# One channel group of the last convolution span moved to GpSimd, and the work between projections and attention put in another order

## The reference, cut to what matters

```python
mod = silu(c) @ ada_w + ada_b                    # 6 x 1024: shift1, scale1, gate1, shift2, scale2, gate2
h = rms_norm(x, norm_mix) * (1 + scale1) + shift1
q, k, v, u = split(h @ w_in)                     # 8 query heads, 2 key heads, head size 64
q, k = apply_rope(rms_norm(q)), apply_rope(rms_norm(k))
attn_out = softmax(q k^T / 8) v
val, gate = split(u); a = val * sigmoid(gate)
y = depthwise_conv(a, conv_w) + conv_b           # 512 channels, 31 taps
conv_out = silu(layer_norm(y, conv_ln_g, conv_ln_b))
x = x + gate1 * (concat([attn_out, conv_out]) @ w_out)
x = x + gate2 * expert_choice_ffn(rms_norm(x, norm_ffn) * (1 + scale2) + shift2)   # 16 experts
```

## Time and profile before

| what | us |
|---|---|
| runs of the kernel, median of 3 (lowest, highest) | 1512.67 (1510.94, 1512.75) |
| the profiled execution, its own time | 1508.8 |
| its span, first to last instruction | 1507.0 |
| PE busy | 1418.2 (94%) |
| DVE busy | 1106.1 (73%) |
| ACT busy | 798.6 (53%) |
| POOL busy | 209.9 (14%) |

### The profile page before, as it was taken

One profiled execution on the slowest core, in us unless ns is written; L12 is line 12 of the kernel. 1 busy time (PEld: TensorE's weight loads), 2 busy tenths in 40 slices (PEclk: granted clock), 3 DMA queues, 4 the chain that ended last, 5 costly groups with the idle time before them and its releaser, 6 DMA issues.

```text
span 1507.0 us, 26861 instructions
## 1 busy us (share of the span) xinstructions
PE 1418.2 (94%) x9933; PEld 1066.8 (71%) x9933; DVE 1106.1 (73%) x1564; ACT 798.6 (53%) x1303; POOL 209.9 (14%) x211
## 2 busy tenths in 40 slices
PE   4999999978999998998499999999999999999996
PEld 1777787636887886876277777777777777777774
DVE  1258888988877887437678887778877787877884
ACT  2222222136777775223556766566665666756662
POOL 0022022100000000211102111221012210212110
PEclk8999999989999999999599999999999999999998
DMA  9400001273000001333888888989889898889951
GB/s 361 153 1 28 29 1 56 98 293 114 2 2 2 2 2 56 112 131 130 300 303 295 299 296 289 317 290 305 287 301 313 290 308 283 304 290 315 308 186 18
DMA packets 113682, 281.31 MB, mean 187 GB/s; under 512 B 10581, under 2 KB 16825, under 8 KB 110552
## 3 DMA queue, kind: packets, MB, share of 16 engines
q1 hardware_dynamic: 105944, 259.54, 48.2%
q0 software_dynamic: 7680, 20.98, 6.0%
HBM read 259.51 MB, written 20.97 MB: 186 GB/s over the span
## 4 chain that ended last, share of the span: by engine, by line
PE 88%; DVE 5%; DMA 2%; ACT 1%; POOL 1%; SPq 1%; issue 1%; DVEq 0%; ACTq 0%; POOLq 0%
PE banks L1455 12%; PE banks L1460 12%; PE banks L1456 12%; PE banks L1480 12%; PE banks L1135 9%; PE banks L1338 6%; PE banks L1146 6%; PE banks L1287 4%; PE banks L1262 4%; PE banks L1272 4%; DVE c_t L1677 2%; DMA ada<-in_ada_w 1%; PE banks L1510 1%; PE banks L1487 1%; PE banks L1299 1%; DMA xn_sample<-xn 1%
## 5 line engine op out<-in xcount | busy, mean ns | idle before, releaser
L2003 DVE TENSOR_TENSOR low<-raw,high 128x1024 fp32r<-128x1024 f32 x384 | 446.5, 1218 | 1.0
L985 ACT ACTIVATE high<-raw 128x1024 fp32r<-128x1024 f32 x384 | 380.4, 1051 | 9.6 <-issue 8.8
L1677 DVE SCALAR_TENSOR_TENSOR c_t<-a_t,taps,c_t 128x256 f32<-128x256 f32 (+2 forms) x360 | 215.0, 660 | 0.5
L1455 PE MATMUL banks<-high,x_hi 128*128 128x512 f32 x512 | 207.9, 406 | 0.0
L1456 PE MATMUL banks<-high,x_lo 128*128 128x512 f32 x512 | 200.5, 392 | 0.0
L1460 PE MATMUL banks<-low,x_hi 128*128 128x512 f32 x512 | 158.3, 390 | 1.1 <-DVE low L2003 1.1
L1135 PE MATMUL banks<-h_t,w_u 128*128 128x256 f32 x640 | 143.9, 382 | 2.9 <-ACT h_t L735 2.9
L1135 PEld LDWEIGHTS banks<-h_t,w_u 128*128 128x128 f32 x640 | 121.1, 192 | 18.9 <-issue 3.1
L1480 PE MATMUL banks<-raw,xs_t 128*32 128x256 f32 x2048 | 118.3, 383 | 0.0
L1455 PEld LDWEIGHTS banks<-high,x_hi 128*128 128x128 f32 x512 | 96.1, 188 | 31.1 <-issue 13.6
L1775 DVE TENSOR_REDUCE negmax<-banks 128x1 f32<-128x1024 f32 (+1 forms) x80 | 84.9, 1062 | 41.4 <-PE banks L1262 41.2
(11 more groups left out here) (230 smaller groups left out, 2128.2 us busy)
## 6 DMA issues: line engine op xcount, KB each, us to landing
raw<-in_w_gate SPq DMA_DIRECT2D x128, 512.0 KB, 4.2
raw<-in_w_up SPq DMA_DIRECT2D x128, 512.0 KB, 5.3
raw<-in_w_down SPq DMA_DIRECT2D x64, 1024.0 KB, 5.0
ada<-in_ada_w SPq DMA_DIRECT2D x24, 1024.0 KB, 8.6
w_u<-in_w_in SPq DMA_DIRECT2D x4, 1024.0 KB, 18.3
x_in<-in_x_prompt SPq DMA_DIRECT2D x4, 1024.0 KB, 4.9
w_out_sb<-in_w_out SPq DMA_DIRECT2D x1, 4096.0 KB, 13.0
x_again<-in_x_prompt SPq DMA_DIRECT2D x4, 1024.0 KB, 5.9
```

The source lines that it names most:

```text
L985: act.activation(high[c % RING][:, :], raw[ph][:, k, :], ACT.Copy).then_inc(hi_ready, 1)
L1455: pe.matmul(bank(b + h), s_hi_k, w_high[:, half], start=(k == 0), stop=False)
L1677: dve.scalar_tensor_tensor(out=c_t[s][:, c, :], in0=a_t[:, c, bass.ds(k + o, n)], scalar=taps[:, c, bass.ds(k, 1)], in1=c_t[s][:, c, :], o ...
L2003: dve.tensor_tensor(low[ph][:, k, :], raw[ph][:, k, :], high[c % RING][:, :].bitcast(F32), ALU.subtract).then_inc(lo_ready, 1)
```

## The change

Four edits.

1. **GpSimd takes channel group 3 of span 2.** All 31 taps of that group leave DVE. POOL makes the first with one TENSOR_SCALAR, then each of 30 taps with two instructions: a TENSOR_SCALAR product into a new buffer `tap_of` and a TENSOR_TENSOR addition to `c_t`. The products start when set 2's products are done (`rows_ready` 3, since `tap_of` takes the place of a load buffer). DVE keeps 93 of 124 tap instructions of span 2. `mean(2)` waits for POOL's last addition.
2. **12 taps ahead instead of 28.** DVE makes AHEAD = 4 taps of 3 groups in the passage; 81 are left for the attention's 16 prompt steps.
3. **The last query turnings are spread** between the adaLN products and the statistics on PE, and the high and low halves are spread on ACT and DVE to match; two low halves stand before the last addition of the rotation. `copy_rows(1)` moves ahead on ACT.
4. **The second `scores` no longer stands behind `mod_turn(2)`**, which moves behind the first turning of the probabilities; DVE's `mod_cols(2)` moves behind the third maximum.

The rest (semaphores merged into `fills_made`, `inv_t` at another address) moves no instruction.

```diff
@@ gpsimd
+            pool.wait_ge(rotated, NT)
+            pool.wait_ge(u_gated, CC * NPAIR)
+            pool.wait_ge(cols_ready, 2)
+            o, n = SPANS[2]
+            c = CC - 1
+            pool.tensor_scalar(c_t[2][:, c, :], a_t[:, c, o:o + n], taps[:, c, 0:1], cols[:, ROW_CB + c:ROW_CB + c + 1],
+                               ALU.mult, ALU.add).then_inc(conv_last, 1)
+            pool.wait_ge(rows_ready, 3)
+            for k in range(1, TAPS):
+                pool.wait_ge(conv_last, 2 * k - 1)
+                pool.tensor_scalar(tap_of[:, :], a_t[:, c, o + k:o + k + n], taps[:, c, k:k + 1], None, ALU.mult).then_inc(conv_last, 1)
+                pool.wait_ge(conv_last, 2 * k)
+                pool.tensor_tensor(c_t[2][:, c, :], c_t[2][:, c, :], tap_of[:, :], ALU.add).then_inc(conv_last, 1)
@@ scalar
+            for i in range(3):
+                high_out(NPAIR - 1, 0, i)
             squares(0)
+            copy_rows(1)
+            for i in range(3):
+                high_out(NPAIR - 1, 1, i)
             squares(1)
             root(0)
             root(1)
-            copy_rows(1)
@@ tensor
-            turn_last_q()
-            mean(1)
-            for k in range(2, 4):
+            turn_q(NPAIR - 1, 0, 0)
+            turn_q(NPAIR - 1, 0, 1)
+            for k in range(2, 6):
                 mod_step(1, k, ada2[k], 2)
-            variance(0)
-            for k in range(4, 6):
-                mod_step(1, k, ada2[k], 2)
-            variance(1)
+            turn_q(NPAIR - 1, 0, 2)
             for k in range(6, KC):
                 mod_step(1, k, ada2[k], 2)
+            pe.wait_ge(qkv_copied, 2 * NT)
+            mean(1)
+            turn_q(NPAIR - 1, 1, 0)
+            turn_q(NPAIR - 1, 1, 1)
+            variance(0)
             mod_turn(1, 7)
+            turn_q(NPAIR - 1, 1, 2)
+            for k in range(2):
+                mod_step(2, k, ada2[k], 3)
+            variance(1)
...
             scores(0)
-            pe.wait_ge(mod_ready, 2)
-            mod_turn(2, 7)
+            pe.wait_ge(rows_copied, 3)
             scores(1)
...
                     turn_probs(n + h, h, nt)
+                    if s == 0 and h == 0:
+                        pe.wait_ge(mod_ready, 2)
+                        mod_turn(2, 7)
@@ vector
                 for i in before_sum:
                     low_out(NPAIR - 1, 0, i)
                 dve.wait_ge(rot1_ready, 2 * q + 2)
...
+            low_out(NPAIR - 1, 0, 2)
+            centre(0)
+            low_out(NPAIR - 1, 1, 0)
+            low_out(NPAIR - 1, 1, 1)
+            centre(1)
+            low_out(NPAIR - 1, 1, 2)
...
-            AHEAD = 7
-            centre(0)
-            some_taps(2, 0, 2 * CC)
-            centre(1)
+            AHEAD = 4
+            some_taps(2, 0, 2 * TAP_COLS[2])
             scale_span(0)
-            some_taps(2, 2 * CC, 5 * CC)
+            some_taps(2, 2 * TAP_COLS[2], AHEAD * TAP_COLS[2])
             dve.wait_ge(rows_turned, 2)
             mod_cols(1)
             scale_span(1)
-            some_taps(2, 5 * CC, AHEAD * CC)
```

More of the change, by code:

```diff
@@ L169, in encoder_layer @@
     inv_rows = put("inv_rows", [P, 2, P], F32, Z1 + 77824)
[L170 to L172 removed]
+    sums = put("sums", [P, 2, QPK], F32, Z1 + 78848)
+    inv = put("inv", [P, 2, QPK], F32, Z1 + 78880)
+    inv_t = put("inv_t", [QPK, P], F32, at["small"] + 8192 + D)
+    tap_of = put("tap_of", [P, SPANS[2][1]], F32, Z1 + 79360)
     sq_c = [put(f"sq_c{i}", [P, CC, SPANS[i][1]], F32, o) for i, o in enumerate((Z1 + 16384, Z1 + 20480, Z1 + 45056))]
@@ L1194, in _ @@
             pe.wait_ge(u_gated, CC * NPAIR)
[L1195 to L1199, removed]
             def mean(s):
                 for c in range(CC):
-                    pe.wait_ge(conv_done[s], CC * (TAPS - 1) + c + 1)
+                    if c < TAP_COLS[s]:
+                        pe.wait_ge(conv_done[s], TAP_COLS[s] * (TAPS - 1) + c + 1)
+                    else:
+                        pe.wait_ge(conv_last, 2 * TAPS - 1)
                     for b, c0, c1 in STAT_BANK[s]:
@@ L1658, in qk_norm @@
                     dve.tensor_tensor(rot1[:, h0:h0 + nh, :], qk[a][:, h0:h0 + nh, :], tab, ALU.mult).then_inc(rot1_ready, 1)
+                for i in before_sum:
+                    low_out(NPAIR - 1, 0, i)
                 dve.wait_ge(rot1_ready, 2 * q + 2)
@@ L1682, in some_taps @@
                 for i in range(first, last):
-                    tap(s, i % CC, i // CC)
+                    tap(s, i % TAP_COLS[s], i // TAP_COLS[s])
             BESIDE = 40
@@ L1733, in _ @@
                 beside(p, 35, BESIDE)
-                qk_norm(2 * p + 1)
-            for a in range(2):
-                for i in range(3):
-                    low_out(NPAIR - 1, a, i)
+                qk_norm(2 * p + 1, (0, 1) if p == NPAIR - 1 else ())
             def centre(s):
@@ L1812, in _ @@
             maximum_of(1)
-            dve.wait_ge(rows_turned, 3)
-            mod_cols(2)
-            dve.wait_ge(mod_ready, 3)
-            scale_of(a2, ROW_NFFN, SCALE2)
             for s, (j, t, t0, nt, l) in enumerate(steps):
@@ L1822, in step_taps @@
                         first, last = (LATE * (3 * (PROMPT_TILES * j + l) + i) // (3 * PROMPT_STEPS) for i in (m, m + 1))
-                        some_taps(2, CC * AHEAD + first, CC * AHEAD + last)
+                        some_taps(2, TAP_COLS[2] * AHEAD + first, TAP_COLS[2] * AHEAD + last)
                 maximum_of(n + 2)
+                if s == 0:
+                    dve.wait_ge(rows_turned, 3)
+                    mod_cols(2)
+                    dve.wait_ge(mod_ready, 3)
+                    scale_of(a2, ROW_NFFN, SCALE2)
                 if s >= 2:
```

37 lines of the change are left out of this document (17 added, 20 removed).

## The result

The changed kernel takes **1502.12 us** (median of 4, 1498.67 to 1502.61) against 1512.71 for the kernel before: a ratio of 0.993, interval 0.9916 to 0.9944. In a second set (e11) it was 1501.27 against 1512.85, 0.9933 (0.992 to 0.9947). One execution of the kernel before (e9) had a mean granted clock of 0.837, took 1661.77 us and is left aside.

A forecast was written before the change was run, and what follows sets the result against it. PE was taken to bound the attention and DVE's taps the passage ahead of it. Lead 8.7 less 1.2 less 3.2 gives 4.3 us faster: 1508.4 us against the median 1512.67, range 1504.0 to 1518.5.

The forecast's parts named there:

- the passage: Ahead of the attention, where DVE's taps bound the kernel: first maximum near 337 us, first exponent near 340.5.
- the lead: Gain ahead of the attention from fewer DVE taps: first exponent 9 us sooner, less 0.3 for a short stop, 8.7 us.
- the meeting: At the passage's end the four scalings of span 1 meet POOL's chain once and wait: 1.2 us lost.
- The step that failed: In the attention, DVE's waits for GpSimd let 0.4 us per prompt step through to PE: 3.2 us over 8 steps.
- The first rival: In the attention no wait reaches PE if additions are nearer 1.25 us: 8.0 us faster, 1504.6; chance 0.16.
- The second rival: In the attention GpSimd gets in at every boundary, second taps pay too: 2.1 us per step, 5.8 slower, 1518.5; chance 0.26.
- 0.53 us of mean wait per tap: DVE taps in the attention: above this mean wait, 2.67 / 5.06, the second rival was to hold.
- The prices on GpSimd: POOL's chain: product 0.8 us (bounds 0.29 and 1.25), addition 1.5, a tap 2.45, 30 taps 74 us.
- From the profile to the median: Whole kernel: 4.3 us gain taken from the 1508.8 us profile, 3.9 below the median 1512.67, applied to that median.

The follow-up runs named there:

- e11: The changed kernel run again, nothing altered, for a second profile and more runs: 1501.27 us, ratio 0.9933 to the kernel before.
- e9: The kernel before run again for another profile, nothing altered: mean granted clock 0.837, 1661.77 us, left aside.
- e1: Changed kernel without GpSimd's 30 products and 30 additions, so the output lacks them; only its first tap stays: 1501.37 us, 0.9926 to the kernel before.
- e7: Changed kernel with GpSimd's product given a second operation, a multiplication by a column of ones: 1505.78 us, 0.9967 to the kernel before.
- e10: The kernel before run again for a third profile, nothing altered: 1513.03 us, one run.
- e8: Changed kernel with GpSimd on channel group 1, six DVE taps in the wait for the last turnings, GpSimd's chain behind the last scaling: 1499.14 us, 0.9918.
- e4: Changed kernel with GpSimd's products held until DVE has made the last scaling of span 1: 1502.53 us, 0.9935 to the kernel before.

## Why the prediction was wrong

**Right: the passage.** Its parts came as forecast, in the first profile's time (changed kernel less the 1.26 us of its later start): last load at 329.6 (near 330), first scores done at 333.5 (near 333), first maximum at 338.2 (337 and 1.2 for the scalings; these lost 1.9, and without POOL's products, in e1, it comes at 336.2). DVE waited 4.4 us for the last halves (4.9). The first exponent stands at 340.8, 0.9 ahead of the forecast (340.5 and 1.2), and what ended ACT's wait is `copy_rows` and the table load.

**Undersized: the lead.** The forecast had 8.7 less 1.2, 7.5 us; at the 80th exponent it is 8.9. e1 shows the lead without the chain as 10.2 us and the meeting as 1.3: the first exponent came 10.5 us sooner there, where the forecast had 9.1, and 0.3 of it was given back, as forecast. Of the 1.4 us that were missing 0.5 are the shorter wait for the last halves.

**The step that failed:** "Such waits come in lumps ahead of a maximum, so I take 0.4 us per step through to PE", 3.2 us. e1 measures it as nothing: from the 5th exponent to the 49th the chain adds 0.00 us. The sum ahead of it came out: 2.4 us of waits per step were forecast and 5.06 x 0.40 = 2.0 measured, against 2.67 of spare time. But this was in part luck, as the product was sized wrong and second taps of a pair wait too (below). The allowance on top had no row behind it: DVE still stood idle for 3.1 of 42 us (378 to 420), and PE not at all. The first rival (8.0 faster) came nearest, and its argument, that the spare time covers the mean wait, holds; but its condition, an addition nearer 1.25 us, doesn't (1.55). I gave it the least chance. With this term at nothing the forecast would have been 7.5 us faster, 1505.2, inside the range; that the result lies below the range takes the 1.4 us of the lead and the last point of this section too.

**The second rival's mechanism is real, its price was too high.** POOL does get in between two taps: with a product pending, the second tap of a pair took 1.42 us rather than 0.88 (at 401.18). And the point that the prediction gave, 0.53 us of mean wait per tap, parts the patterns of five taps in a step: 0.40 with DVE idle at times, 0.64 with DVE full. Yet the second pattern costs 1.2 to 1.7 us and not 13.3. It was priced at 2.1 us per step, where 12.24 less 11.98 is 0.26 at most.

**The prices on GpSimd were wrong, and it didn't matter.** The addition took 1.55 (1.5 forecast). The product took 1.88, outside the bounds of 0.29 and 1.25; a tap took 3.6 us in place of 2.45, and the chain some 118 us rather than 74. It had the time. That the product blocks DVE for only some 0.8 us of its 1.9 leaves DVE free for the rest; e7, where products are shorter and additions come sooner, is the slower one.

**From the profile to the median.** The forecast took its gain from a profile that stood 3.9 us below the median, and moved it to the median as it was. That profile is a short execution of this kernel: e10, near the median, loses 2.7 us behind the mark that it doesn't. The two profiles of the changed kernel are 9.9 to 10.5 us shorter than e10 from the mark to the end, and 7.1 to 7.7 shorter than the first profile. Up to the 80th exponent, where e10 loses 1.2, the difference is the clock behind PE's long stop. The granted clock is 0.50 for the 3.0 us behind it in the first profile (350.9 to 353.9), for 5.9 us in e10 (352.4 to 358.3) and for 3.6 us in the changed kernel (340.8 to 344.4); there it was at 0.50 in the last 3 us of the stop already, when PE had nothing to do. So some 1.2 of the 10.6 us are a loss of the kernel before that its first profile doesn't show. The rest of e10's loss lies behind the 80th exponent, and the changed kernel has it too: the variance of span 2, which runs at half of the clock, takes 6.02 us in the first profile, 6.88 in e10 and 6.79 in the changed kernel, and a stretch at 712 to 760 us has a granted clock of 0.64, 0.61 and 0.61 (702 to 750 us in the changed kernel). So the ninth slice of the first profile's page isn't the only slow one behind the start-up in the first half: the twentieth has 0.59 (716 to 753 us).

## What to carry to other kernels

When work is moved to an engine that a busy one has to wait for, multiply the wait per instruction by the instructions per step and compare it with the spare time in the step: below it the cost was nothing here. Look at the first steps by themselves: one tap more in a step cost 4 us, all in the first two, where DVE had no time over. Two engines that ran in loops fell into a repeating pattern, and the pattern that one build showed wasn't the only one: shift the start by an instruction or two and look again before trusting it. Take an engine's work from the stage in which it ends last, and look at what it then waits for: filling that 4.4 us wait (e8) gave another 3 us (3.2 at the 80th exponent against e4, which has the same late start).

## What was not expected of the hardware

- On GpSimd a TENSOR_SCALAR with one operation took 1.88 us for 128x640, with two operations 0.87 to 0.88 (first tap, e7). Why isn't known.
- Of the 1.88 us only about 0.8 kept DVE's taps waiting, while an addition kept them until its end, 1.55 us.
- DVE and POOL locked into one of two patterns, 0.40 or 0.64 us of wait per tap, the same one for dozens of instructions and the same again in a second execution (e11).
